# A head's loads in another order, cached keys on a semaphore of their own, value outputs copied in the MLP

## The chip, the cores and the metric

The kernel runs on one core of a Trainium2 chip. A core has five engines with instruction queues of their own: TensorE (PE, matrix products and transposes), VectorE (DVE), ScalarE (ACT), GpSimd (POOL) and SyncE (SP, which here only issues DMAs). They meet through semaphores. The metric is the device time of one launch in microseconds; the median of the runs before is 2062.98 us.

## What is computed

One layer of a streaming encoder, for a prompt of 1024 rows and a sample of 8 sequences with 16 new rows each, which share the weights. Four groups of four attention heads read the same projection; an output projection, an MLP and a gated embedding follow. Cut to the parts that the change touches:

```python
def _layer(h, p_l, past, ...):
    xn = _rmsnorm(h, g_attn)
    aq, ak, av, bq, bk, bv, cq, ck, cv, dq, dk, dv, dlogf = _project(xn, w_in, b_f)
    # past is None for the prompt; for the sample, cached keys and values stand in front:
    a_k = jnp.concatenate([a_past[:, :, 0], ak], axis=1)      # so for A, C, D; B has a window of 128
    a_v = jnp.concatenate([a_past[:, :, 1], av], axis=1)
    a_out = _stick_breaking(aq, a_k, a_v, q_pos, k_pos)        # A
    b_out = _swa_sample(bq, b_k, b_v, ..., sinks, rel_bias)    # B: softmax with a sink and a bias table
    c_out = _diff_attention(cq, c_k, c_v, ..., lam, rel_bias)  # C: two softmax maps and a bias table
    d_out = _forgetting_attention(dq, d_k, d_v, ..., f_q, f_k) # D: gates f added to the scores
    h = h + jnp.concatenate([a_out, b_out, c_out, d_out]) @ w_out
    h = h + jnp.square(jax.nn.relu(_rmsnorm(h, g_mlp) @ w_up)) @ w_down
    h = h + jax.nn.sigmoid(h @ w_ple_gate) * (p_l @ w_ple_proj)
    state = (stack([ak, av]), last window of [bk, bv], stack([ck, cv]), stack([dk, dv]), dlogf)
    return h, state
```

The new keys and values are outputs too (`a_kv_prompt`, `a_kv_sample` and so on); B's sample buffer is the old window moved on by 16 rows.

## The kernel before

The 1024 + 128 rows make nine tiles of 128 rows; the ninth is the sample. The program is a row of blocks, with a barrier of all engines between them: the projection, attention, the output projection, the MLP, the gated embedding. The projection leaves the turned queries and keys in DRAM, each as a high and a low part (`q2`, `k2`, cached keys `kc2`), and the values as rows (`vrows`).

Attention is a loop of two passes (`heads_loop`). A pass has eight jobs, `JOBS`: two heads each of A, B, C and D, an even and an odd one; a job has nine tiles. PE runs one tile ahead with the scores (`scores`), then turns the weights of the tile before, then multiplies by the values of the one before that. Each engine goes through its own list; what is not ready holds up all that stands behind it on that engine.

SP loads what a head needs into one of two buffers (`x = job % 2`), and starts when all outputs of the head two before are computed (L917). Its list for a head is, before the change: keys `k_turned` and queries `q_turned` in four arrangements, cached keys `k_sample_turned` (six and two loads; twelve and four for C, whose heads have two halves), with an even head the values `v_rows` and `v_cache_rows` of both heads of the group (semaphores `v_in`), and at the end the small ones: for B and C the bias of the prompt, eight loads of 9 KB with the sample's bias and one scalar a head (`head_scalar`); for D two loads of gates and eight of the sample's gates. All but the values count on one semaphore, `job_in0` or `job_in1`; `loads(g)` says how many there are. Three engines wait for its full count with `job_loaded`: DVE at the end of the seventh step of the head before (`bias`, or for D `sample_gates`), PE at a head's first scores, and GpSimd before it spreads the sample's queries and new keys (`spread_operands`).

Before the loop DVE casts two constants and clears two buffers (semaphore `att_zeros_set`), and GpSimd raises each of the loop's semaphores by one and then `att_primed`. SP and PE wait for both.

GpSimd also copies the new values from `vrows` to the outputs, DRAM to DRAM: nine copies a pass (`copies`), two behind a job's spreading. In the MLP it has nothing to do. There PE alternates products with `w_up` and `w_down`; SP loads their slots of 256 KB into four raw buffers, ACT and DVE split each into a high and a low part.

Of the kernel before, what the change touches and what calls it, by code (L numbers as in the profile page):

```python
# [19 lines left out]
F32 = mybir.dt.float32  # L20
# [5 lines left out]
P = 128  # L26
D = 1024
SEQ = 1024
# [4 lines left out]
HD = 64  # L33
# [29 lines left out]
def encoder(nc, i, o):  # L63
    with ExitStack() as ctx:
# [630 lines left out]
        with ExitStack() as mem:  # L695
            def sb(name, shape, dt=F32):
# [30 lines left out]
            a_set, kv_out = sem("att_zeros_set"), sem("kv_rows_out")  # L727
# [4 lines left out]
                "job_in0": "loads of the even head", "job_in1": "loads of the odd head",  # L732
                "turned": "PE: a bank of transposes is full", "v_in0": "loads of the values of a pair of heads of A or C",
# [80 lines left out]
            def loads(g):  # L814
                return (16 if g == "C" else 8) + {"A": 0, "B": 10, "C": 10, "D": 2 + DEC_B}[g]
# [14 lines left out]
            per["job_in1"] = 16 * sum(loads(g) for g, _ in JOBS[1::2])  # L830
            per.update({f"read{x}": len(range(x, len(ORDER), 3)) for x in range(3)})
# [71 lines left out]
            with nc.Block() as block:  # L903

                @block.sync
                def _(sp):
                    sp.wait_ge(primed_sem, 1)
                    sp.wait_ge(a_set, 4)

                    def body(j):  # L910
                        for job, (g, e) in enumerate(JOBS):
# [6 lines left out]
                            for m in range(HD // half):  # L918
                                own, at_hi, at_lo = bass.ds(HD * h + half * m, half), 2 * half * m, 2 * half * m + half
                                of_k = bass.ds(HD * kvh + half * m, half)  # L920
                                for part, to in ((0, at_hi), (1, at_lo)):
                                    sp.dma_start(kt[to:to + half, x, :].bitcast(F32), k2[g][part][of_k, :]).then_inc(done, 16)
                                    sp.dma_start(qt[0][to:to + half, x, :].bitcast(F32), q2[g][part][own, :]).then_inc(done, 16)
                                for part, to in ((1, at_hi), (0, at_lo)):
                                    sp.dma_start(qt[1][to:to + half, x, :].bitcast(F32), q2[g][part][own, :]).then_inc(done, 16)
                                for part, to in ((0, at_hi), (1, at_lo)):
                                    sp.dma_start(ks[to:to + half, x, :, 0:n].bitcast(F32),
                                                 kc2[g][part][of_k, :].rearrange("p (b n) -> p b n", b=DEC_B)).then_inc(done, 16)
                            if e == 0:
                                v, nb = GROUPS.index(g) % 2, DEC_B * cached(g)  # L930
                                w = HD if g == "B" else P
                                cache = i[f"cache_{g.lower()}_kv"]
                                vcol = 128 if g == "B" else 256
                                sp.wait_ge(q["o_full"], at("o_full", TILES * (job_of(GROUPS[GROUPS.index(g) - 2], 1) + 1) - (0 if g in "CD" else NT)))
                                sp.dma_start(vr[:, v, :, 0:w], vrows[:, bass.ds(V_COL[g] + w * j, w)].rearrange("(t p) d -> p t d", p=P)).then_inc(q[f"v_in{v}"], 16)
                                sp.dma_start(vc[:, v, 0:nb, 0:w], cache[:, bass.ds(vcol + w * j, w)].rearrange("(s p) d -> p s d", p=P)).then_inc(q[f"v_in{v}"], 16)
# [9 lines left out]
                            if g == "D":  # L946
                                sp.dma_start(cs[x][:, :], fcum_p[bass.ds(h, 1), :].partition_broadcast(P)).then_inc(done, 16)
                                sp.dma_start(fq[:, x, :], fcum_q[bass.ds(h, 1), :, :].rearrange("o p t -> (o p) t")).then_inc(done, 16)
                                for b in range(DEC_B):
                                    own = slice(b * DEC_S, (b + 1) * DEC_S)  # L950
                                    sp.dma_start(bs[own, x, :], fcum_s[b, bass.ds(h, 1), :].partition_broadcast(DEC_S)).then_inc(done, 16)
# [961 lines left out]
```

## Time and profile before

| | |
|---|---|
| runs | 2061.21, 2062.98, 2066.68 us; median 2062.98 us |
| the profiled execution | 2077.38 us, span 2075.8 us, mean granted PE clock 0.900 |
| busy in the span | PE 1839.8 us (89%), DVE 850.9 (41%), ACT 646.8 (31%), POOL 90.6 (4%) |
| DMA | 195.33 MB, 94 GB/s over the span |
| projection | to 338 us |
| attention, first pass | 366 to 656 us: PE busy 218.16 of 290 us, granted clock 0.69 |
| attention, second pass | 656 to 980 us: PE busy 246.18 of 324 us, granted clock 0.76 |
| MLP | 1123 to 1916 us |

The span runs from the first to the last instruction; the execution's own time is 1.6 us longer. The profiled execution is 14.4 us above the median of the runs without a profile. A row of the timeline gives in brackets how long its engine had been idle and what ended that. SPq is SP's queue: the time of such a row is that of the issue, not of the transfer; when the data has landed stands in the rows on DMA issues.

### The profile page before, as it was taken

Reading aid. Unit: us, or ns where it says so; the run is one execution under the profiler, and the core shown is the slowest. Engines: PE = TensorE matmul, PEld = TensorE weight load, DVE = VectorE, ACT = ScalarE, POOL = GpSimd, SP = SyncE. Lnnn points to the kernel's source line nnn. Section 1 sums busy time; section 2 is a strip of 40 time slices with the busy share of each in tenths; the row PEclk is TensorE's granted clock in tenths of the full one; section 3 lists DMA queues with packets and bytes.
Section 4 is the critical chain, followed back from the end, with each engine's and each line's share of the span. In section 5 each row is a group of like instructions: output and inputs, shape, how many; then the busy total and the mean of one; then the engine's idle time right before and its main releaser. Section 6 shows DMA issues by size and latency. Waiting matters only on the chain. (4 is left out here: it accounts for less than half of the span.)

```text
span 2075.8 us, 28346 instructions
## 1 busy us (share of the span) xinstructions
PE 1839.8 (89%) x10134; PEld 1659.4 (80%) x10134; DVE 850.9 (41%) x1619; ACT 646.8 (31%) x1387; POOL 90.6 (4%) x178
## 2 busy tenths in 40 slices
PE   6999995774888684788798999999999999999898
PEld 6999984674778574678688989999898999988686
DVE  4333322662455662455444333333333333333334
ACT  5322311552334552334223222222121212211326
POOL 0000000000011000010100000000000000000000
PEclk9999997676569686679899999999999999999899
DMA  5676733455347356354521111111111111110202
GB/s 170 211 245 221 250 140 77 106 120 125 65 106 162 77 115 133 65 114 93 191 95 36 41 50 47 52 49 46 45 41 41 41 41 41 41 41 21 87 28 94
DMA packets 152405, 195.33 MB, mean 94 GB/s; under 512 B 43188, under 2 KB 106356, under 8 KB 152248
## 3 DMA queue, kind: packets, MB, share of 16 engines
q1 hardware_dynamic: 105352, 131.63, 24.1%
q10 hardware_dynamic: 39136, 36.05, 5.3%
q0 software_dynamic: 7776, 25.76, 3.9%
q8 instruction: 88, 1.44, 0.3%
q14 instruction: 53, 0.43, 0.1%
HBM read 143.17 MB, written 54.81 MB: 95 GB/s over the span
## 5 line engine op out<-in xcount | busy, mean ns | idle before, releaser
L113 PE MATMUL up<-xt_hi,w_hi_even 128*128 128x384 f32 x768 | 258.2, 336 | 1.9 <-PEq L1426 1.8
L114 PE MATMUL up<-xt_lo,w_hi_even 128*128 128x384 f32 x768 | 257.8, 336 | 0.0
L115 PE MATMUL up<-xt_hi,w_lo_even 128*128 128x384 f32 x768 | 257.7, 336 | 0.0
L115 PE MATMUL down<-w_hi_odd_b,hidden_lo 128*128 128x512 f32 x576 | 224.6, 390 | 0.0
L114 PE MATMUL down<-w_lo_odd_b,hidden_hi 128*128 128x512 f32 x576 | 224.6, 390 | 0.0
L113 PE MATMUL down<-w_hi_odd_b,hidden_hi 128*128 128x512 f32 x576 | 224.2, 389 | 0.0
L1338 PE MATMUL scores<-k_turned,q_turned_straight 128*128 128x512 f32 (+5 forms) x224 | 87.7, 518 | 121.8 <-ACT probs L1060 68.8
L1633 DVE TENSOR_TENSOR h_rows<-down,h_rows 128x1024 f32<-128x1024 f32 x72 | 88.2, 1224 | 236.2 <-PE down L115 236.2
L1373 PE MATMUL outs<-v_rows,probs_turned 128*128 128x64 f32 x984 | 153.1, 307 | 35.0 <-DVE probs_turned L901 30.0
L1373 PEld LDWEIGHTS outs<-v_rows,probs_turned 128*128 128x128 f32 x984 | 145.5, 226 | 47.3 <-DVE head_out L1227 30.4
L1598 ACT ACTIVATE hidden_rows<-up 128x384 f32<-128x384 f32 x96 | 47.3, 492 | 417.2 <-PE up L115 417.2
L1338 PEld LDWEIGHTS scores<-k_turned,q_turned_straight 128*128 128x128 f32 (+1 forms) x224 | 44.1, 256 | 133.5 <-issue 72.1
L113 PEld LDWEIGHTS up<-xt_hi,w_hi_even 128*128 128x128 f32 x768 | 145.0, 189 | 3.8 <-DVE xt_lo L140 2.2
L114 PEld LDWEIGHTS up<-xt_lo,w_hi_even 128*128 128x128 f32 x768 | 144.9, 189 | 0.8
L1626 DVE TENSOR_TENSOR hidden_rows<-hidden_rows 128x384 f32<-128x384 f32 x96 | 53.6, 558 | 224.2 <-ACT hidden_rows L1598 224.2
L115 PEld LDWEIGHTS up<-xt_hi,w_lo_even 128*128 128x128 f32 x768 | 144.9, 189 | 0.0
L115 PEld LDWEIGHTS down<-w_hi_odd_b,hidden_lo 128*128 128x128 f32 x576 | 108.2, 188 | 22.5
L114 PEld LDWEIGHTS down<-w_lo_odd_b,hidden_hi 128*128 128x128 f32 x576 | 108.1, 188 | 22.0
L113 PEld LDWEIGHTS down<-w_hi_odd_b,hidden_hi 128*128 128x128 f32 x576 | 108.2, 188 | 21.9
L901 ACT COPY probs_turned<-turns 128x512 f32<-128x512 f32 (+3 forms) x156 | 68.3, 459 | 159.6 <-PE turns L1357 159.0
L1357 PE MATMUL turns<-cst,probs 128*128 128x128 f32 x520 | 101.9, 325 | 1.6 <-ACT probs L1046 1.6
L1177 DVE TENSOR_REDUCE stats<-scores 128x1 f32<-128x272 f32 (+8 forms) x76 | 51.5, 705 | 89.1 <-PE scores L1342 88.6
(262 smaller groups left out, 3539.4 us busy)
## 6 DMA issues: line engine op xcount, KB each, us to landing
w_raw<-w_up SPq DMA_DIRECT2D x64, 256.0 KB, 2.9
w_raw<-w_down SPq DMA_DIRECT2D x64, 256.0 KB, 3.0
w_raw<-w_in SPq DMA_DIRECT2D x24, 256.0 KB, 4.6
head_rows<-head_out ACTq DMA_DIRECT2D x16, 288.0 KB, 5.1
head_rows_in<-head_rows POOLq DMA_DIRECT2D x9, 512.0 KB, 4.7
x_rows<-x_prompt SPq DMA_DIRECT2D x8, 512.0 KB, 3.7
w_raw<-w_out SPq DMA_DIRECT2D x16, 256.0 KB, 5.0
residual_rows<-x_prompt POOLq DMA_DIRECT2D x16, 256.0 KB, 3.2
```

The source lines that it names most:

```text
L113: nc.tensor.matmul(out, xh, wh, start=first, stop=False)
L114: nc.tensor.matmul(out, xh, wl, start=False, stop=False)
L115: return nc.tensor.matmul(out, xl, wh, start=False, stop=last)
L901: copy(pt[i % 2][:, b * P:b * P + k], TB[n % 3][:, 0:k]).then_inc(q[f"read{n % 3}"], 1)
L1177: nc.vector.tensor_reduce(st_[:, col:col + 1], src[:, 0:n], AX.X, ALU.max, negate=True).then_inc(q["m_ready"], 1)
L1338: nc.tensor.matmul(S[UNIT[(i, m)] % 2][:, c:c + w], qt[part][own, e, P * t:P * (t + 1)], kt[own, e, k0 + c:k0 + c + w], start=part == 0, s ...
L1357: last = nc.tensor.transpose(TB[n % 3][:, (y - b) * P:(y - b + 1) * P], block_src, ident)
L1373: last = nc.tensor.matmul(dst, w[:, y * P:(y + 1) * P], vr[:, e, first_block(i) + y, own], start=y == 0, stop=y == nb - 1)
L1598: nc.scalar.activation(R[:, f % 2, :], U[f][:, 0:GT], ACT.Relu).then_inc(relu_d, 1)
L1626: nc.vector.tensor_tensor(R[:, f % 2, :], R[:, f % 2, :], R[:, f % 2, :], ALU.mult).then_inc(sq_d, 1)
L1633: nc.vector.tensor_tensor(H[:, t, :], DN[t % 2][:, :], H[:, t, :], ALU.add).then_inc(dn_add, 1)
```

## The change

SP's list for a head has a new order: the small loads first (bias and scalar, or gates), then keys and queries, then with an even head the values, and the cached keys last. The cached keys count on semaphores of their own, `ks_in0` and `ks_in1`. Only PE waits for these, before a head's sample tile; `loads(g)` loses their number, so DVE, GpSimd and PE at the head's start wait without them. SP no longer waits for `att_zeros_set`; GpSimd does, before its first spread. GpSimd's nine copies a pass become nine copies of whole tensors at the start of the MLP's block, and it waits for them at that block's end.

```diff
@@ per, semaphores @@
+                "ks_in0": "cached keys of the even head", "ks_in1": "cached keys of the odd head",
             def loads(g):
-                return (16 if g == "C" else 8) + {"A": 0, "B": 10, "C": 10, "D": 2 + DEC_B}[g]
+                return (12 if g == "C" else 6) + {"A": 0, "B": 10, "C": 10, "D": 2 + DEC_B}[g]
+            def cache_loads(g):
+                return 4 if g == "C" else 2
@@ SP @@
                     sp.wait_ge(primed_sem, 1)
-                    sp.wait_ge(a_set, 4)
...
                             sp.wait_ge(q["o_full"], at("o_full", TILES * (job - 1)))
-                            for m in range(HD // half):
-                                (keys, queries, then cached keys ks, all .then_inc(done, 16))
-                            if e == 0:
-                                (values)
                             if g in "BC":
                                 (bias of the prompt, of the sample, scalar)
                             if g == "D":
                                 (gates)
+                            for m in range(HD // half):
+                                (keys, queries, .then_inc(done, 16))
+                            if e == 0:
+                                (values)
+                            for m in range(HD // half):
+                                of_k, at_hi, at_lo = ...
+                                for part, to in ((0, at_hi), (1, at_lo)):
+                                    sp.dma_start(ks[to:to + half, x, :, 0:n].bitcast(F32),
+                                                 kc2[g][part][of_k, :].rearrange("p (b n) -> p b n", b=DEC_B)).then_inc(q[f"ks_in{x}"], 16)
@@ GpSimd in attention @@
                     pool.sem_inc(primed_sem, 1)
+                    pool.wait_ge(a_set, 4)
+                    pool.sem_inc(pool_passed, 1)
-                    def copies(j):
...
-                            for dst, src in rows_out[2 * job:2 * job + 2]:
-                                nc.gpsimd.dma_start(dst, src).then_inc(kv_out, 16)
-                    pool.wait_ge(kv_out, 2 * 16 * 9)
@@ PE, scores @@
                         if is_sample(i):
                             pe.wait_ge(q["spread"], at("spread", 3 * (job + 1)))
+                            pe.wait_ge(q[f"ks_in{e}"], at(f"ks_in{e}", 16 * sum(cache_loads(JOBS[x][0]) for x in range(e, job + 1, 2))))
@@ MLP @@
+                @block.gpsimd
+                def _(pool):
+                    for g in "ACD":
+                        own = slice(V_COL[g], V_COL[g] + 256)
+                        nc.gpsimd.dma_start(o[f"{g.lower()}_kv_prompt"][:, 256:512], vrows[0:SEQ, own]).then_inc(kv_out, 16)
+                        nc.gpsimd.dma_start(o[f"{g.lower()}_kv_sample"][:, 256:512], vrows[SEQ:SEQ + P, own]).then_inc(kv_out, 16)
+                    own = slice(V_COL["B"], V_COL["B"] + P)
+                    (b_kv_prompt from vrows, b_kv_sample from cache_b_kv and from vrows)
+                    pool.wait_ge(kv_out, 16 * 9)
```

SP at the start of attention, before: it waits for the cleared buffers and for the primer, then loads the first head of A, cached keys included.

```order
L843 UNCONDITIONAL_BRANCH [waits att_zeros_set,att_primed]
L843 ISA
L922 ISA [waits att_o_full]
L922 DMA k_turned<-k_turned_A_hi 64x1152
L923 DMA q_turned_straight<-q_turned_A_hi 64x1152
L922 DMA k_turned<-k_turned_A_lo 64x1152
L923 DMA q_turned_straight<-q_turned_A_lo 64x1152
L925 DMA q_turned_crossed<-q_turned_A_lo 64x1152
L925 DMA q_turned_crossed<-q_turned_A_hi 64x1152
L927 ISA
L927 DMA k_sample_turned<-k_cache_turned_A_hi 64x8x256
L927 DMA k_sample_turned<-k_cache_turned_A_lo 64x8x256
```

And now: it waits for the primer alone, and the values follow the queries.

```order
L848 UNCONDITIONAL_BRANCH [waits att_primed]
L848 ISA
L941 ISA [waits att_o_full]
L941 DMA k_turned<-k_turned_A_hi 64x1152
L942 DMA q_turned_straight<-q_turned_A_hi 64x1152
L941 DMA k_turned<-k_turned_A_lo 64x1152
L942 DMA q_turned_straight<-q_turned_A_lo 64x1152
L944 DMA q_turned_crossed<-q_turned_A_lo 64x1152
L944 DMA q_turned_crossed<-q_turned_A_hi 64x1152
L950 REGISTER_ALU
L951 ISA [waits att_o_full]
```

The wait for `att_zeros_set` is gone, and the two loads of `k_sample_turned` stand behind the values.

SP at the second head of B, before: the end of its list, from the second load of queries on, with the bias and the scalar at the end.

```order
L923 DMA q_turned_straight<-q_turned_B_hi 64x1152
L922 DMA k_turned<-k_turned_B_lo 64x1152
L923 DMA q_turned_straight<-q_turned_B_lo 64x1152
L925 DMA q_turned_crossed<-q_turned_B_lo 64x1152
L925 DMA q_turned_crossed<-q_turned_B_hi 64x1152
L927 DMA k_sample_turned<-k_cache_turned_B_hi 64x8x128
L927 DMA k_sample_turned<-k_cache_turned_B_lo 64x8x128
L940 ISA
L940 DMA bias_prompt<-bias_rows 128x256
L943 DMA bias_sample<-bias_rows 16x144 x8
L945 REGISTER_ALU
L945 DMA head_scalar<-swa_sinks 128x1
```

And now, from the bias on:

```order
L925 DMA bias_prompt<-bias_rows 128x256
L928 DMA bias_sample<-bias_rows 16x144 x8
L930 REGISTER_ALU
L930 DMA head_scalar<-swa_sinks 128x1
L941 DMA k_turned<-k_turned_B_hi 64x1152
L942 DMA q_turned_straight<-q_turned_B_hi 64x1152
L941 DMA k_turned<-k_turned_B_lo 64x1152
L942 DMA q_turned_straight<-q_turned_B_lo 64x1152
L944 DMA q_turned_crossed<-q_turned_B_lo 64x1152
L944 DMA q_turned_crossed<-q_turned_B_hi 64x1152
L956 DMA k_sample_turned<-k_cache_turned_B_hi 64x8x128
L956 DMA k_sample_turned<-k_cache_turned_B_lo 64x8x128
```

Ten small loads have moved in front of the six of keys and queries, and the cached keys to the end.

PE before the sample tile of the first head of A, before:

```order
L1373 MATMUL outs<-v_rows,probs_turned 128x64 x4
L1309 ISA
L1320 REGISTER_ALU [waits att_spread]
L1329 MATMUL scores<-k_sample_turned,q_sample_spread_straight 128x272 [waits att_a_logw]
L1329 MATMUL scores<-k_sample_turned,q_sample_spread_crossed 128x272
```

And now:

```order
L1363 MATMUL outs<-v_rows,probs_turned 128x64 x4
L1298 ISA
L1299 ISA [waits att_spread]
L1310 REGISTER_ALU [waits att_ks_in0]
L1319 MATMUL scores<-k_sample_turned,q_sample_spread_straight 128x272 [waits att_a_logw]
L1319 MATMUL scores<-k_sample_turned,q_sample_spread_crossed 128x272
```

One wait more stands in front of the tile's first product.

## Rows read from the trace of the kernel before

**Rows 1.** Waits of the whole run: who waited <- for whom: us, times, longest.

```profile
PE scores L1338 <- ACT probs L1060: 68.8, 28, 20.6
...
DVE bias_sample L1139 <- DMA head_scalar<-rel_bias: 37.2, 2, 20.0
...
PE scores L1338 <- DMA k_sample_turned<-k_cache_turned_A_lo: 28.2, 1, 28.2
...
PE scores L1338 <- DVE bias_prompt_lo L1146: 15.6, 2, 8.4
...
DVE bias_sample L1123 <- DMA bias_sample<-fcum_sample: 13.5, 2, 7.2
```

**Rows 2.** Stretches: their us, engines' busy us (x), PE clock, DMA share, GB/s.

```profile
510.00:556.00 46.00, 36.91 (x174) 31.40 (x176) 22.51 (x59) 15.94 (x43) 2.28 (x6) 0.50 0.39 84
...
1123.00:1916.00 793.00, 792.93 (x4023) 724.47 (x4024) 274.22 (x391) 167.23 (x320) 0.00 (x0) 1.00 0.13 43
```

**Rows 3.** Timeline, start of attention: start us, us, engine, line, operation [idle before].

```profile
347.66 1.98 DVE L1115 MEMSET q_sample_spread_crossed<- 128x2304 f32 x1 [0.43 <-issue]
...
350.09 0.59 SPq L922 DMA_DIRECT2D k_turned<-k_turned_A_hi  x1
...
353.31 0.55 SPq L925 DMA_DIRECT2D q_turned_crossed<-q_turned_A_hi  x1
...
356.18 5.27 SPq L936 DMA_DIRECT2D v_cache_rows<-cache_a_kv  x1
...
365.99 0.47 PE L1338 MATMUL scores<-k_turned,q_turned_straight 128*128 128x128 f32 x1 [28.16 <-DMA k_sample_turned<-k_cache_turned_A_lo]
...
374.40 0.68 PE L1373 MATMUL outs<-v_rows,probs_turned 128*128 128x64 f32 x2 [1.45 <-DVE probs_turned L901]
```

**Rows 4.** Source line 961, GpSimd's primer: ns, first and last start us.

```profile
L961 POOLq EVENT_SEMAPHORE  x1: 17/17/17, 348.4 to 348.4; - x1
```

**Rows 5.** DMA issues of that start: xcount, KB, us to landing.

```profile
q_turned_crossed<-q_turned_A_hi SPq DMA_DIRECT2D x1, 288.0 KB, 7.4
...
v_cache_rows<-cache_a_kv SPq DMA_DIRECT2D x1, 1024.0 KB, 15.5
```

**Rows 6.** Timeline, first head of C in the first pass.

```profile
480.91 0.32 SPq L922 DMA_DIRECT2D k_turned<-k_turned_C_hi  x1
...
507.12 0.29 DVE L1139 TENSOR_SCALAR bias_sample<-bias_sample,head_scalar 128x144 f32<-128x144 f32 x1 [19.99 <-DMA head_scalar<-rel_bias]
...
509.99 0.47 PE L1338 MATMUL scores<-k_turned,q_turned_straight 64*128 64x128 f32 x2 [20.55 <-ACT probs L1060]
```

**Rows 7.** Timeline and landing, second head of C in the first pass.

```profile
522.65 0.32 SPq L922 DMA_DIRECT2D k_turned<-k_turned_C_hi  x1
...
530.22 0.39 SPq L925 DMA_DIRECT2D q_turned_crossed<-q_turned_C_hi  x1
...
q_turned_crossed<-q_turned_C_hi SPq DMA_DIRECT2D x1, 144.0 KB, 6.5
```

**Rows 8.** Timeline, small loads, second head of C in the second pass.

```profile
845.57 0.42 SPq L940 DMA_DIRECT2D bias_prompt<-bias_rows  x1
...
849.89 0.35 SPq L945 DMA_DIRECT2D head_scalar<-rel_bias  x1
```

**Rows 9.** Timeline, second head of B in the first pass.

```profile
455.93 0.53 SPq L922 DMA_DIRECT2D k_turned<-k_turned_B_hi  x1
...
461.62 0.62 SPq L940 DMA_DIRECT2D bias_prompt<-bias_rows  x1
...
467.23 0.35 SPq L945 DMA_DIRECT2D head_scalar<-swa_sinks  x1
...
471.87 0.15 DVE L1136 TENSOR_SCALAR head_scalar_negated<-head_scalar 128x1 f32<-128x1 f32 x1 [9.34 <-DMA head_scalar<-swa_sinks]
```

**Rows 10.** DMA issues of the whole run: xcount, KB each, median us to landing.

```profile
a_kv_prompt<-value_rows POOLq DMA_DIRECT2D x2, 512.0 KB, 4.0
```

**Rows 11.** Timeline of ACT, first split of `w_down` in the MLP.

```profile
1143.39 1.14 ACT L106 CAST w_hi_odd_b<-w_raw 128x512 fp32r<-128x512 f32 x2
```

More of the change, by code:

```diff
@@ L830, in encoder @@
             per["job_in1"] = 16 * sum(loads(g) for g, _ in JOBS[1::2])
+            def cache_loads(g):
+                return 4 if g == "C" else 2
+            per.update({f"ks_in{x}": 16 * sum(cache_loads(g) for g, _ in JOBS[x::2]) for x in range(2)})
             per.update({f"read{x}": len(range(x, len(ORDER), 3)) for x in range(3)})
@@ L917, in body @@
                             sp.wait_ge(q["o_full"], at("o_full", TILES * (job - 1)))
-                            for m in range(HD // half):
[L919 to L928, printed above, removed]
-                            if e == 0:
[L930 to L936, printed above, removed]
                             if g in "BC":
@@ L951, in body @@
                                     sp.dma_start(bs[own, x, :], fcum_s[b, bass.ds(h, 1), :].partition_broadcast(DEC_S)).then_inc(done, 16)
+                            for m in range(HD // half):
+                                of_q, at_hi, at_lo = bass.ds(HD * h + half * m, half), 2 * half * m, 2 * half * m + half
+                                of_k = bass.ds(HD * kvh + half * m, half)
+                                for part, to in ((0, at_hi), (1, at_lo)):
+                                    sp.dma_start(kt[to:to + half, x, :].bitcast(F32), k2[g][part][of_k, :]).then_inc(done, 16)
+                                    sp.dma_start(qt[0][to:to + half, x, :].bitcast(F32), q2[g][part][of_q, :]).then_inc(done, 16)
+                                for part, to in ((1, at_hi), (0, at_lo)):
+                                    sp.dma_start(qt[1][to:to + half, x, :].bitcast(F32), q2[g][part][of_q, :]).then_inc(done, 16)
+                            if e == 0:
+                                v, nb = GROUPS.index(g) % 2, DEC_B * cached(g)
+                                w = HD if g == "B" else P
+                                cache = i[f"cache_{g.lower()}_kv"]
+                                vcol = 128 if g == "B" else 256
+                                sp.wait_ge(q["o_full"], at("o_full", TILES * (job_of(GROUPS[GROUPS.index(g) - 2], 1) + 1) - (0 if g in "CD" else NT)))
+                                sp.dma_start(vr[:, v, :, 0:w], vrows[:, bass.ds(V_COL[g] + w * j, w)].rearrange("(t p) d -> p t d", p=P)).then_inc(q[f"v_in{v}"], 16)
+                                sp.dma_start(vc[:, v, 0:nb, 0:w], cache[:, bass.ds(vcol + w * j, w)].rearrange("(s p) d -> p s d", p=P)).then_inc(q[f"v_in{v}"], 16)
+                            for m in range(HD // half):
+                                of_k, at_hi, at_lo = bass.ds(HD * kvh + half * m, half), 2 * half * m, 2 * half * m + half
+                                for part, to in ((0, at_hi), (1, at_lo)):
+                                    sp.dma_start(ks[to:to + half, x, :, 0:n].bitcast(F32),
+                                                 kc2[g][part][of_k, :].rearrange("p (b n) -> p b n", b=DEC_B)).then_inc(q[f"ks_in{x}"], 16)
                     heads_loop(sp, body)
@@ L1011, in body @@
                     def body(j):
-                        rows_out = list(copies(j))
                         for job in range(len(JOBS)):
```

18 lines of the change are left out of this document (6 added, 12 removed).

## The prediction, made before the changed kernel was run

> **What bounds the kernel now.** I read the waits first, for the whole run, because they say where TensorE (PE) stands still and what released it. In the MLP there is nothing to win: from 1123 to 1916 us PE is busy in 792.93 of 793.00 us at the full granted clock [rows 2]. The idle time lies in the attention stage, and three rows hold the long pieces [rows 1]: 28.2 us at its start, once, until a load of cached keys had landed; 15.6 us in two waits on the bias tiles; and 68.8 us behind ACT's exponentials, of which one wait alone is 20.6 us. DVE's own rows tell what stands behind the last two: it waits 37.2 us, twice, for C's `head_scalar`, the last load of a head, and 13.5 us, twice, for the gates of D.
>
> Then the timelines, to see which load ends each wait. At the start, SP's first issue (350.09) comes 0.45 us behind the end of DVE's second memset (347.66 + 1.98 = 349.64), and PE starts at 365.99 [rows 3]. At the first head of C, SP issues from 480.91 on, DVE gets through its wait of 19.99 us at 507.12, PE moves at 509.99 after 20.55 us [rows 6]. At the second head of B SP issues from 455.93, DVE goes on at 471.87 after 9.34 us [rows 9]. The rule behind all: DVE, GpSimd and PE wait for one semaphore that counts all loads of a head, and a head's first issue waits until the head two before it is done. After that first issue, only the order and length of the load list decide. So I price each place as "first issue to ready", before and after.
>
> **Part 1, the start.** Six loads of keys and queries are issued first; the last, at 353.31, takes 7.4 us to land: 360.7 [rows 3, 5], 10.6 us after the first issue. PE waited on until the cached keys had landed, 365.99, so the new semaphore takes 5.2 us off. SP no longer waits for the memsets, but for GpSimd's primer, which signals at 348.4 [rows 4]; with the same 0.45 us and two more increments in front I take 1.0 us earlier. Gain 6.2 us (5.2 if the memset was no gate, 6.4 if the increments cost nothing). What is late next: the values. `v_cache_rows`, issued at 356.18, landed 15.5 us later at 371.7 behind 1 MB of cached keys; without these (5.2 us) and 1.0 us earlier it lands at 365.5, and PE's first value product, at 374.40, moves to 368.2 [rows 3, 5]. 2.7 us to spare. The cached keys then land some 5 us after the values, and their tile is the ninth of the head: covered. The wait that GpSimd takes over lies before its first spread, which needs the queries anyway.
>
> **Part 2, first head of C, in both passes.** Before: ready 507.12 - 480.91 = 26.2 us after the first issue [rows 6]. After: ten small loads in front, then twelve of keys and queries. The small ones are priced by their issue: 849.89 + 0.35 - 845.57 = 4.7 us where the queue took them at once [rows 8], 467.23 + 0.35 - 461.62 = 6.0 us in the slower place [rows 9]. I take 5.3, because the queue is empty now but ACT's store of an earlier head is issued in the same microseconds. The twelve: the second head of C took from 522.65 to 530.22 + 6.5 = 536.7, 14.1 us, with one pair of cached keys among them [rows 7]. Such a pair of 256 KB is half of what took 5.2 us at the start, 2.6, so 11.5 us; up to 12.7 if the store slows them. New: 5.3 + 11.5 = 16.8 us against 26.2: 9.4 us. The second pass waited 37.2 - 20.0 = 17.2 us instead of 20.0 [rows 1], so I take 8.6 there. Together 18.0. PE's wait falls from 20.55 to some 11 us and does not vanish. Late next: values (1.6 MB, 8 us at the pace of 1 MB of cached keys in 5.2) land near 25 us after the first issue; PE wants them two tiles into the head, so they stay covered, and cached keys eight tiles in.
>
> **Part 3, second head of B, in both passes.** Before: 471.87 - 455.93 = 15.9 us [rows 9]. Here the small loads were issued under the transfers of the keys; in front, they stand alone. New: 5.3 + 10.6 (six loads as at the start; 11.3 at worst beside the store) = 15.9 to 16.6. A loss of 0.2 each, -0.4 us; the cached keys left out are 2 us that the small loads eat.
>
> **Part 4, the rest.** D: DVE's two waits of some 7 us [rows 1] stand in front of the maximum of a tile that PE is still working on, and PE's own waits list none behind them; 0 to 1 us, I take 0.5 for both. First head of B, second of A and of C: the waits come in twos, one a pass [rows 1], and none is theirs: nothing to gain, and part 3's 0.7 us more would not hurt. PE's added wait, 16 times, is a register instruction and a semaphore read: 0.5 us against. GpSimd's 18 copy issues in attention held up nobody that PE waits for: 0. The nine copies now start with the MLP. A copy of 512 KB landed in 4.0 us [rows 10]; 4480 KB make 35 us if one follows another. In these 35 us only `w_down` loads are needed, and the first split of them is at 1143.39, 20 us into the MLP [rows 11]: cover for a load that takes twice its time. If the next four come 3 us late too, ACT catches up in its idle time; bounds 0 to 6 us against, and I take 0, because PE reaches the first down product only after eight units of the up product.
>
> **Sum.** 6.2 + 18.0 - 0.4 + 0.5 - 0.5 = 23.8 us off the profiled execution's 2077.38: 2053.6. The runs shown have a median 0.7% below it (2062.98), so 2053.6 x 0.993 = **2039 us**, 1.2% faster. With the small loads at 4.7 or 6.0 us and the twelve at 12.7 this case reaches from 2036 to 2045.
>
> **Rivals.** Let b be the time by which the small loads hold up the keys; the sum above has b = 5.3 at four places (C and B, two passes each), so the gain is 23.8 + 4 x 5.3 - 4b = 45 - 4b.
>
> *The small loads cost more than their issue*: b = 8, for tiny rows that hold the queue. Gain 13, 2050 us. For it: from their first issue to the end of DVE's wait there were 10.25 us (461.62 to 471.87) [rows 9]. Against it: they stood behind 2.2 MB of keys, queries and cached keys there.
>
> *Slower: the small loads go one after another*, each paying its own way to landing before the keys move. The mechanism sits in SP's queue at every head of B, C and D; the point from which it decides is b = 11.3, where 45 - 4b is zero. One small load costs between 0.47 us (4.7 / 10, nothing but its issue) and 4.6 us (from the last issue, 467.23, to the end of DVE's wait, 471.87) [rows 8, 9]; at 2 us each ten make b = 20: 45 - 80, 35 us slower, 2098, with D's share not counted. Against it: ten are issued in 6.0 us, and 4.6 us after the last one all had landed [rows 9]; in a row that would leave a load 1.1 us. This is also where the Trainium skill speaks against the change: "DMA: Bandwidth & Descriptors", "Rules for kernel authors", says that transfers under 64 KB pay mostly overhead, and its section on the anatomy of one DMA fits a fixed cost of about 2 us to each (on GpSimd's path; these loads are SP's). Paid in a row, that would be this rival's 2098; the trace bears out an overhead in latency, not one that adds up.
>
> *The wait is only replaced*: C becomes ready earlier, but PE then stands for values, cached keys or the bias work on DVE, and only the start pays: 2057. Against: the cover worked out above.
>
> *The clock*: the head of C runs with the low level granted (0.50 over 510 to 556, PE busy 36.91 of 46 us) [rows 2]. If a wait of 11 us instead of 20 leaves it high for half of that head, some 4 us a head more, and the same at other places: 2031. Against: the wait stays long, and the head's own pauses, 9 of these 46 us, stay as they are.
>
> **Chances.** Forecast 0.70, dear small loads 0.14, clock 0.08, wait replaced 0.05, slower 0.03. The range 2030 to 2053 leaves out the last two and the far half of the second, some 0.15. What a measurement of this kernel can tell from no change is about 0.3%, 6 us, so faster means under 2057: 0.70 + 0.14 + 0.08 = 0.92; within 0.3% 0.05; slower 0.03.
>
> **What would show it.** SP's first issue near 349, PE's start near 359.8, released by queries and not by cached keys. DVE's wait for C near 10 us instead of 20 and 17; its wait at B still 9 us. PE's idle before the sample tiles not released by cached keys. PE as busy in the MLP as before. Wrong would be: keys that land later than 17.5 us after the first issue at C or 17 at B; values that end a wait of PE at the start; a gap in the MLP's first 40 us.

## The result, and the profile after

| | before | changed |
|---|---|---|
| median of 12 runs each on one chip | 2070.32 us (2059.40 to 2077.18) | 2049.65 us (2042.48 to 2056.34) |
| profiled execution | 2077.38 us | 2052.67 us |

The ratio is 0.991, 95% interval 0.989 to 0.9929: some 19 us, with 15 to 23 in the interval. The forecast was 2039 us and 23.8 us off the profiled execution; the pair of profiled executions lies 24.7 us apart, of which 1.7 us are the projection, which the change leaves alone (it ends at 336.16 instead of 337.83 us).

The waits of the changed kernel (who waited <- for whom: us, times, longest) answer to [rows 1]:

```profile
PE scores L1328 <- ACT probs L1049: 53.4, 28, 11.4
...
PE scores L1328 <- DMA q_turned_crossed<-q_turned_A_hi: 21.9, 1, 21.9
DVE bias_sample L1128 <- DMA q_turned_crossed<-q_turned_C_hi: 21.7, 2, 10.9
...
PE scores L1328 <- DVE bias_prompt_lo L1135: 14.2, 2, 7.1
...
DVE bias_sample L1112 <- DMA q_turned_crossed<-q_turned_D_hi: 4.9, 2, 2.5
```

Where a row names a load, the name has changed: what is last now are the queries, not the cached keys or the small loads. C's wait on DVE went from 37.2 to 21.7 us, D's from 13.5 to 4.9, PE's start from 28.2 to 21.9, and B's stayed (15.6 to 14.2).

The start, in the changed kernel's timeline and DMA issues (xcount, KB, us to landing), answers to [rows 3, 5]:

```profile
345.98 1.98 DVE L1104 MEMSET q_sample_spread_crossed<- 128x2304 f32 x1 [0.43 <-issue]
347.25 0.59 SPq L941 DMA_DIRECT2D k_turned<-k_turned_A_hi  x1
...
358.11 0.47 PE L1328 MATMUL scores<-k_turned,q_turned_straight 128*128 128x128 f32 x1 [21.95 <-DMA q_turned_crossed<-q_turned_A_hi]
...
366.54 0.68 PE L1363 MATMUL outs<-v_rows,probs_turned 128*128 128x64 f32 x2 [1.45 <-DVE probs_turned L906]
...
v_cache_rows<-cache_a_kv SPq DMA_DIRECT2D x1, 1024.0 KB, 12.0
...
q_turned_crossed<-q_turned_A_hi SPq DMA_DIRECT2D x1, 288.0 KB, 7.5
```

SP issues 0.7 us before the second memset has ended, not behind it. PE's first value product waits 1.45 us for DVE, to the hundredth as before: the cached values, issued at 351.91 and landed 12.0 us later at 363.9, came in time.

The first head of C and the second of B in the first pass (timeline), which answer to [rows 6, 9]:

```profile
477.61 0.35 SPq L925 DMA_DIRECT2D bias_prompt<-bias_rows  x1
...
483.04 0.38 SPq L941 DMA_DIRECT2D k_turned<-k_turned_C_hi  x1
...
494.53 0.29 DVE L1128 TENSOR_SCALAR bias_sample<-bias_sample,head_scalar 128x144 f32<-128x144 f32 x1 [10.87 <-DMA q_turned_crossed<-q_turned_C_hi]
...
497.39 0.48 PE L1328 MATMUL scores<-k_turned,q_turned_straight 64*128 64x128 f32 x2 [11.43 <-ACT probs L1049]
...
452.61 0.36 SPq L925 DMA_DIRECT2D bias_prompt<-bias_rows  x1
...
468.95 0.15 DVE L1125 TENSOR_SCALAR head_scalar_negated<-head_scalar 128x1 f32<-128x1 f32 x1 [8.02 <-DMA q_turned_crossed<-q_turned_B_hi]
```

C is ready 494.53 - 477.61 = 16.9 us after its first issue (forecast 16.8, before 26.2), B 468.95 - 452.61 = 16.3 (forecast 15.9 to 16.6, before 15.9). The small loads hold up the keys' first issue by 483.04 - 477.61 = 5.4 us at C (forecast 5.3; the same in the second pass) and by 5.8 and 5.7 at B.

A part of C's 26.2 us before is seen in SP's queue. There the small loads stood behind the load of 1 MB of cached values, and the first of them alone took 8 us to issue (7.81 in the second pass), against 0.35 now:

```profile
492.68 8.01 SPq L940 DMA_DIRECT2D bias_prompt<-bias_rows  x1
```

The MLP (windows: us, busy us of PE, PEld, DVE, ACT, POOL, clock, DMA share, GB/s), and its slowest copy:

```profile
1097.40:1891.00 793.60, 793.57 (x4026) 725.64 (x4027) 274.00 (x391) 167.08 (x320) 5.55 (x9) 1.00 0.15 49
...
w_raw<-w_down SPq DMA_DIRECT2D x4, 256.0 KB, 5.7
...
b_kv_sample<-value_rows POOLq DMA_DIRECT2D x1, 64.0 KB, 16.8
```

PE is as busy as in [rows 2]; the copies are done within 17 us of their issue, and the first loads of `w_down` beside them took 5.7 us without a gap behind it.

What the forecast has no term for is seen in windows of single heads. Before: the first heads of B in both passes (437 and 756), the first and second of C in the first pass.

```profile
437.20:463.80 26.60, 22.36 (x177) 21.30 (x175) 15.25 (x49) 11.82 (x38) 2.37 (x6) 0.87 0.34 86
488.40:559.00 70.60, 40.95 (x209) 35.09 (x207) 24.82 (x69) 16.97 (x47) 2.36 (x6) 0.53 0.50 105
559.00:610.30 51.30, 43.12 (x269) 37.91 (x267) 25.79 (x67) 18.88 (x52) 5.55 (x8) 0.63 0.45 102
755.90:778.10 22.20, 20.54 (x177) 19.44 (x175) 12.41 (x48) 11.41 (x38) 2.37 (x6) 0.92 0.45 114
```

The same four heads in the changed kernel:

```profile
429.50:462.20 32.70, 29.34 (x177) 28.61 (x175) 15.40 (x49) 11.56 (x38) 1.18 (x4) 0.63 0.15 34
484.90:543.50 58.60, 36.31 (x208) 31.43 (x207) 24.78 (x69) 17.00 (x47) 1.16 (x4) 0.62 0.63 132
543.50:591.20 47.70, 39.19 (x269) 34.44 (x267) 25.66 (x67) 18.91 (x52) 4.87 (x7) 0.71 0.49 108
733.30:765.90 32.60, 29.25 (x176) 28.52 (x175) 15.34 (x49) 11.57 (x38) 1.16 (x4) 0.63 0.16 34
```

The first head of B issues the same products, with 3.4 us of pauses in both passes against 4.2 and 1.7 before, but at a clock of 0.63 instead of 0.87 and 0.92: 6.1 and 10.4 us longer. C's heads run at a higher clock than before: without the wait, 70.60 - 20.55 = 50.1 us became 58.60 - 11.43 = 47.2 (in the second pass 49.5 became 47.2), and the second head's 51.30 became 47.70 (in the second pass it took 47.5 both times). Over attention both nearly cancel: without PE's idle time it took 469.3 us before and 470.8 after (from PE's first scores to its last output, less the idle time in front of each of its instructions in the timeline), while the idle time in it fell from 150.7 to 132.8.

### The profile page after: what moved, and what is told of

Read it like the earlier page. It is cut to its first block and busy times, and to the rows that moved or that the text cites. A ratio compares the mean times of both kernels' runs of the same rounds, so it can differ in the third digit from the quotient of the medians.

```text
span 2050.9 us, 28291 instructions
## 1 busy us (share of the span) xinstructions
PE 1840.6 (90%) x10134; PEld 1664.0 (81%) x10134; DVE 850.9 (41%) x1619; ACT 647.1 (32%) x1387; POOL 85.2 (4%) x169
## 3 DMA queue, kind: packets, MB, share of 16 engines
q1 hardware_dynamic: 105352, 131.63, 24.7%
## 5 line engine op out<-in xcount | busy, mean ns | idle before, releaser
L1363 PEld LDWEIGHTS outs<-v_rows,probs_turned 128*128 128x128 f32 x984 | 152.1, 235 | 44.1 <-DVE head_out L1216 27.8
L1363 PE MATMUL outs<-v_rows,probs_turned 128*128 128x64 f32 x984 | 158.8, 315 | 32.3 <-DVE probs_turned L906 27.4
L113 PEld LDWEIGHTS down<-w_hi_odd_b,hidden_hi 128*128 128x128 f32 x576 | 108.2, 188 | 21.9
```

Of the source, the lines that this page charges most:

```text
L113: nc.tensor.matmul(out, xh, wh, start=first, stop=False)
L1363: last = nc.tensor.matmul(dst, w[:, y * P:(y + 1) * P], vr[:, e, first_block(i) + y, own], start=y == 0, stop=y == nb - 1)
```

## The experiments

PE's four long waits are given for the second head of B and the first of C, each in the first and second pass. Ratios are to the kernel before, run beside each kernel on the same chip. There it took 2068.5 us (e1 to e4), 2065.7 (e5, e6, e7, e10), 2073.0 (e9, e11, e12) and 2067.0 (e13), so kernels of different groups are compared by their ratios and not by their medians.

| kernel | median us | ratio, interval | waits at B | at C |
|---|---|---|---|---|
| before | 2070.3 | 1 | 8.4, 7.2 | 20.6, 17.8 |
| changed | 2049.7 | 0.991, 0.989 to 0.9929 | 7.1, 7.0 | 11.4, 11.4 |
| e1 small loads last | 2061.2 | 0.997, 0.9946 to 0.9994 | 6.5, 7.8 | 19.5, 20.1 |
| e2 small loads in front, nothing else | 2068.8 | 0.9996, 0.9973 to 1.0019 | 10.7, 10.9 | 17.4, 15.3 |
| e3 copies in attention | 2043.8 | 0.9868, 0.9837 to 0.990 | 7.1, 6.9 | 11.6, 11.4 |
| e4 keys, then small | 2034.5 | 0.9818, 0.9787 to 0.9849 | 4.2, 6.0 | 8.8, 8.7 |
| e5 merged small loads | 2041.7 | 0.9883, 0.9844 to 0.9923 | 6.9, 4.3 | 6.2, 9.7 |
| e6 small loads' own semaphore | 2042.9 | 0.9895, 0.9862 to 0.9928 | 7.5, 5.2 | 8.9, 6.4 |
| e7 merged, own semaphore | 2035.9 | 0.9862, 0.9826 to 0.9897 | 4.9, 2.7 | 5.5, 7.0 |
| e9 keys, merged small, own semaphore | 2029.7 | 0.9817, 0.9781 to 0.9853 | 5.7, 3.3 | 7.0, 6.9 |
| e10 eight small loads more | 2058.4 | 0.9956, 0.9931 to 0.9981 | 11.2, 10.5 | 10.8, 11.0 |
| e11 unread products in the waits | 2048.4 | 0.9898, 0.9866 to 0.993 | 6.3, 6.0 | 6.2, 5.5 |
| e12 and in C's tiles | 2026.9 | 0.9796, 0.9759 to 0.9833 | 4.5, 6.3 | 6.1, 6.1 |
| e13 = e9 with those of C's tiles | 2009.2 | 0.9715, 0.9672 to 0.9759 | 4.8, 5.2 | 7.3, 7.0 |

**Which part pays: e1 and e2.** e1 is the changed kernel with the blocks of SP's list in another order:

```diff
-  small loads; keys and queries; values; cached keys
+  keys and queries; values; cached keys; small loads
```

> The changed kernel with the small loads put back to the end of a head's list (keys and queries, values, cached keys, small loads); start, semaphores and copies stay as changed. My theory (the order of the small loads pays at C, the start pays by the semaphore): PE starts as in the changed kernel, 21.9 us after the projection; at the first head of C all loads are in some 26 us after the first issue instead of 16.9, PE's wait there goes from 11.4 back to 18 to 21 us in both passes; B a little better than before (15.5 to 16). Time 6 to 8 us below the kernel before, 14 to 17 above the changed one, near 2064. Rival (the cached keys on a semaphore of their own are what pays at C, the place of the small loads does not matter): PE's wait at C stays near 11 us and the time within 4 us of the changed kernel.

e2 is the kernel before with the block `if g in "BC" ... if g == "D" ...` put in front of the keys.

> The kernel before with only the small loads put in front of a head's list; one semaphore, cached keys behind the keys, start and copies as before. My theory: PE's start as before (28 us); at the first head of C ready at 5.3 + 14.1 + 2.6 = 22 us after the first issue instead of 26, at the second head of B 5.3 + 10.6 + 2.6 = 18.5 instead of 15.9; the two nearly cancel, time 0 to 6 us below the kernel before. Rival (putting the small loads in front is the whole gain outside the start): 10 us or more below the kernel before, C ready at 17 to 18.

Waits on DVE in e1, and then in e2:

```profile
DVE bias_sample L1128 <- DMA head_scalar<-rel_bias: 38.4, 2, 19.5
...
DVE head_scalar_negated L1125 <- DMA head_scalar<-swa_sinks: 16.1, 2, 8.7
```

```profile
DVE bias_sample L1139 <- DMA k_sample_turned<-k_cache_turned_C_lo: 31.7, 2, 16.9
...
DVE head_scalar_negated L1136 <- DMA k_sample_turned<-k_cache_turned_B_lo: 23.5, 2, 11.8
```

In e1 C waits as before the change, and what is left is the start: 6 us by the ratio (1 to 11 in the interval), as expected. In e2 C is ready 22.9 us after its first issue (22 expected) and B 18.1 to 18.3 (18.5 expected): PE's wait at C falls by 2.4 to 3.1 us a pass and that at B grows by 2.3 to 3.7, and the sum is nothing. So neither the order of the small loads nor the own semaphore of the cached keys is the gain at C; it takes both, since whatever stands last on the semaphore ends the wait.

**The copies: e3** puts the nine copies a pass back into GpSimd's loop.

> The changed kernel with the value copies put back to GpSimd's list in attention (eighteen halves, two behind a head's spreading). My theory: the copies cost nothing at either place; time within 3 us of the changed kernel, PE's waits at B and C within 0.5 us of it. Rival (the copies' traffic lay on the loads of the heads, and moving them is a part of the gain): 4 to 10 us above the changed kernel, with PE's waits at B or C longer by 1 us or more each.

The four waits are the same within 0.2 us. By the ratios e3 is some 9 us shorter than the changed kernel, known to some 8 (by the two intervals), which neither its theory (within 3 us) nor its rival (longer) had. The waits do not show where that lies, and it stays open. What is shown is that putting the copies back into attention made nothing longer, so that moving them gained nothing.

**The price of the small loads: e4, e5, e10.** e4 changes the order once more; e5 makes one load of eight; e10 makes sixteen of eight at B and C.

```diff
 e4
-  small loads; keys and queries; values; cached keys
+  keys and queries; small loads; values; cached keys
 e5
-  for b in range(DEC_B):
-      sp.dma_start(bs[b * DEC_S:(b + 1) * DEC_S, x, 0:P + DEC_S], src[:, 0:P + DEC_S]).then_inc(done, 16)
+  sp.dma_start(bs[:, x, 0:P + DEC_S], src[:, 0:P + DEC_S].unsqueeze(0).broadcast_to((DEC_B, DEC_S, P + DEC_S))).then_inc(done, 16)
```

> The changed kernel with keys and queries first, then the small loads, then values, then cached keys. My theory (in front the small loads cost their issue time, 5 us, with the transfer engines idle; behind the keys their issue lies under the transfers): ready at B 13 us after the first issue instead of 16.3, at C 14 instead of 16.9; PE's four long waits lose 2 to 3.5 us each; time 8 to 13 us below the changed kernel. Rival (small rows queue behind the keys' data and land late, as at B before the change, 15.9 us): PE's waits within 1 us of the changed kernel, no difference that can be measured.

> The changed kernel with the eight loads of bias_sample made one (for B and C from the same 16 rows, for D from the eight sequences' gates): three small loads a head in front instead of ten. By my formula each place pays b, the issue time of the small loads: 3 x 0.47 = 1.4 us instead of 5.3, so ready at C 13 us after the first issue instead of 16.9, at B 12.4 instead of 16.3; PE's four long waits shrink by 3.5 to 4 us each; about 15 us below the changed kernel, 34 below the kernel before. Rival (the small loads cost latency, not issue time: the keys stand behind the landing of the last one): the wait shrinks by 1.5 us a place at most, 6 us in all. Second rival (one load that reads the same rows eight times is as long as the eight): no difference.

> The changed kernel with bias_sample at B and C loaded in sixteen loads of half the size: eight more issues in front of the keys, the same bytes. By my formula b grows by 8 x 0.47 = 3.8 us at four places: PE's waits at C 15 us, at B 11, 15 us above the changed kernel, near 2064. Rival (the small loads lie beside the keys' transfers and cost latency alone): within 4 us of the changed kernel.

e4's waits on DVE show the small loads last again, but sooner than the keys that stand behind them in the changed kernel:

```profile
DVE bias_sample L1128 <- DMA head_scalar<-rel_bias: 16.3, 2, 8.2
DVE head_scalar_negated L1125 <- DMA head_scalar<-swa_sinks: 11.9, 2, 6.9
```

At C the first issue stands at 473.99 and DVE goes on at 488.44: 14.4 us (expected 14); at B it is 13.9 and 14.3 (expected 13). PE's four waits lose 36.9 - 27.6 = 9.3 us together, and the ratio falls by 0.009, or 19 us, known to some 8: the small loads are better issued under the keys' transfers than ahead of them. They may stand behind the keys, but not behind the values and cached keys: e1, where they do, differs from e4 in that alone, and C is ready after 25.1 and 25.7 us there.

e10 stretches the issue at C from 5.4 to 7.3 us only:

```profile
472.90 0.36 SPq L925 DMA_DIRECT2D bias_prompt<-bias_rows  x1
...
480.21 0.35 SPq L941 DMA_DIRECT2D k_turned<-k_turned_C_hi  x1
...
491.17 0.29 DVE L1128 TENSOR_SCALAR bias_sample<-bias_sample,head_scalar 128x144 f32<-128x144 f32 x1 [10.26 <-DMA q_turned_crossed<-q_turned_C_hi]
```

A load of half the size was issued every 0.37 us instead of 0.46, so eight more cost 2 us and not 3.8. C was ready 491.17 - 472.90 = 18.3 us after its first issue, and 18.6 in the second pass (16.9 in the changed kernel), B 18.5 and 18.7 (16.3): 1.4 to 2.4 us later, where 3.8 were expected. PE's waits do not show this: at B they grew by 3.4 and 4.0 us and at C not at all, because PE ran dry at other moments (at C 10.3 us after the first issue instead of 8.4). By the ratios e10 is some 10 us longer than the changed kernel, known to some 7, between its theory's 15 and its rival's 4.

In e5 C was ready after 13.9 and 15.2 us (13 expected) and B after 13.8 in both passes (12.4 expected): 1.6 to 3.0 us sooner, where 3.9 were expected. The three small loads held up the keys by 1.7 to 2.0 us instead of 1.4, and the keys then took 11.9 to 13.5 us at C, instead of 11.5. The time, some 6 us below the changed kernel and known to some 9, decides between none of e5's three cases. So the formula's sign held at every place in e5 and e10, and its size came out at a third to three quarters. The Trainium skill, "DMA: Bandwidth & Descriptors", "Rules for kernel authors", says to coalesce many small transfers; the waits agree, with 27.1 us for the four in e5 against 36.9, while the interval of e5's ratio takes in the changed kernel's 0.991.

**A semaphore for the small loads: e6, e7, e9.**

```diff
-  .then_inc(done, 16)                    # small loads
+  .then_inc(q[f"sm_in{x}"], 16)
-  job_loaded(dve, job)
+  small_loaded(dve, job)                 # waits for sm_in alone
```

> The changed kernel, in its own order, with the small loads on semaphores of their own, for which alone DVE waits; GpSimd and PE wait for keys and queries as now. Theory: DVE gets through at 7 to 8 us after the first issue instead of 16.9, the bias and the last tile of the head before are done while the keys arrive, and PE starts when they land: its wait at C falls from 11.4 by the 2.9 us between DVE's release and PE's start to 8.5, at B from 7.1 by 1.4 to 5.7; 8 to 9 us below the changed kernel. Rival (what holds PE at C is the exponentials of the head before, not the keys): PE's wait at C falls to 3 us or less, 20 us below.

> Both: three small loads in front on semaphores of their own, keys and queries behind them. Keys land at 1.4 + 11.5 = 13 us after the first issue at C and 12.4 at B; PE runs dry 8.4 and 10.6 us after it, so its waits are 4.5 us at C and 1.8 at B, against 11.4 and 7.1: 4 x 6 = 24 us below the changed kernel, near 2025. Rival (the two gains are one and the same wait): no better than the merged loads alone, 15 us below.

> The order keys and queries, small loads, values, cached keys, with bias_sample in one load and the small loads on semaphores of their own, for which alone DVE waits. Keys land at 10.7 us after the first issue at C, the three small loads just behind them at 11 to 11.5: PE's wait at C 4 to 5 us, at B 1 to 3, against 11.4 and 7.1. About as good as merged small loads in front with their own semaphore, 2028 to 2036; rival (DVE passes its wait only when the last small load has landed, and PE waits for the bias tiles after that): C's wait 7 us or more, 2036 to 2042.

The waits of e6, and then of e7, name the keys' and queries' transfer itself:

```profile
PE scores L1338 <- DMA q_turned_crossed<-q_turned_C_hi: 15.3, 2, 8.9
PE scores L1338 <- DMA q_turned_crossed<-q_turned_B_hi: 12.6, 2, 7.5
...
DVE bias_sample L1138 <- DMA head_scalar<-rel_bias: 2.0, 1, 2.0
```

```profile
PE scores L1335 <- DMA q_turned_crossed<-q_turned_C_hi: 12.6, 2, 7.0
PE scores L1335 <- DMA q_turned_crossed<-q_turned_B_hi: 7.5, 2, 4.9
```

DVE's long waits at C are gone (21.7 us in the changed kernel, 2.0 in e6), and PE's wait there is 8.9 where 8.5 was expected: keys hold PE, not the exponentials behind DVE. In e9 the small loads are last again and DVE's wait at C is back (12.7 us, of which 6.4 at most); PE's four waits sum to 22.9 us in e9 and to 20.1 in e7.

The time followed the waits only roughly. Against the changed kernel, PE's idle time in attention fell by 12.4 us in e6, 17.8 in e7, 18.2 in e9 and 8.2 in e4; by the ratios the time fell by 3, 10, 19 and 19 us, each known to some 8. e6's 3 leaves its 8 to 9 open, e7 stays short of its 24; e9 has the time of its theory, but with the 7 us of wait at C that its rival gave. The idle time is read from one execution, and PE's own time differs beside it. Attention as a whole (windows as above), in the changed kernel, in e6 and in e9:

```profile
358.11:961.63 603.52, 470.75 (x3096) 425.47 (x3096) 328.32 (x799) 263.80 (x648) 33.88 (x76) 0.73 0.49 103
```

```profile
357.35:940.63 583.28, 462.91 (x3096) 415.81 (x3096) 329.54 (x799) 263.23 (x648) 34.14 (x76) 0.75 0.50 107
357.64:934.12 576.48, 461.91 (x3096) 414.13 (x3096) 328.91 (x799) 263.60 (x648) 33.90 (x76) 0.75 0.51 108
```

The same 3096 instructions kept PE busy for 470.75 us at a mean granted clock of 0.73, and for 462.91 and 461.91 us at 0.75. The runs of one kernel differ in the same way: e2's shortest took 2059.38 us at a mean clock of 0.919, its longest 2082.91 at 0.892. So what the waits leave over goes with the clock.

**The clock: e11, e12, e13.** Products of `ident` with `ident`, into a bank of the turns that is free at that moment, which nobody reads:

```diff
+  def idle(i, count):
+      x = WHERE[("tile", max(i - 2, 0), 0)]
+      wait_read(pe, x - 3)
+      for _ in range(count):
+          nc.tensor.matmul(TB[x % 3][:, 0:P], ident, ident, start=True, stop=True, skip_group_check=True)
   def scores(i):
+      if g == "C" and t > 0:                                         # e12, e13
+          idle(i, 3)
+      if t == 0 and (g, e) in (("A", 0), ("B", 1), ("C", 0)):        # e11, e12
+          idle(i, {"A": 24, "B": 12, "C": 24}[g])
```

> The changed kernel with products that nobody reads on PE in its long waits: 24 of 128x128 before the first head of A, 12 before the second of B, 24 before the first of C, into a bank of the turns that is free then (0.27 us each at the full clock, 0.42 at half: 6 to 10 us, within the waits). Nothing else is changed, the waits themselves end when they did. Theory (the rise and fall of the granted clock, set off by the waits, is what moves the rest of attention by 10 to 15 us from run to run and kernel to kernel): the heads behind a filled wait run at a higher clock, 0.62 in the first head of C goes over 0.75, attention without PE's idle time falls from 471 by 8 to 15 us, the total by as much. Rival (a head's clock is set by its own short pauses): 0.55 to 0.68 there again, total within 4 us of the changed kernel.

> The one before with three such products more in front of each tile of C but the first (32 tiles in all, 0.8 us a tile at the full clock, 1.3 at half), where PE pauses 1.1 to 2 us a tile. Theory (a tile's pauses hold the clock of C down): C's heads run at 0.9 to 1.0 instead of 0.62 and 0.71 and take 40 us or less instead of 47 without the long wait: 20 to 30 us less in all for the four. Rival (the clock stays low, the products cost their time beyond the pauses): C's heads are 3 to 8 us longer each, total 10 to 30 us more.

> The kernel with keys and queries first, three small loads on semaphores of their own, values, cached keys, and before each tile of C but the first the three products that nobody reads; none in the long waits. Theory (the products hold the clock of C by themselves, and the two gains lie at different places): C's heads at 0.9 to 1.0 and 5 to 7 us shorter each than without them, in all 20 to 25 us less than the kernel without them (2029.7), 2005 to 2012. Rival (the clock of C was raised by the products in the waits ahead of it): C's heads at 0.6 to 0.7, 10 to 30 us more than without them.

The two heads of C in the first pass, in e11, then e12, then e9, then e13 (windows as above):

```profile
474.60:533.30 58.70, 41.62 (x256) 36.68 (x254) 24.77 (x69) 17.00 (x47) 1.17 (x4) 0.68 0.63 128
533.30:581.00 47.70, 39.19 (x269) 34.43 (x267) 25.65 (x67) 18.90 (x52) 4.89 (x7) 0.71 0.49 108
```

```profile
483.60:534.70 51.10, 38.34 (x304) 34.15 (x303) 24.67 (x69) 17.00 (x47) 1.17 (x4) 0.90 0.72 147
534.70:576.70 42.00, 35.18 (x316) 31.27 (x314) 25.56 (x67) 18.91 (x52) 4.87 (x7) 1.00 0.56 123
```

```profile
472.00:527.10 55.10, 37.82 (x208) 32.52 (x207) 24.76 (x69) 16.97 (x47) 1.16 (x4) 0.60 0.59 122
527.10:574.60 47.50, 39.14 (x269) 34.39 (x267) 25.64 (x67) 18.88 (x52) 4.87 (x7) 0.71 0.51 109
```

```profile
481.10:529.70 48.60, 35.05 (x256) 30.68 (x254) 24.59 (x69) 16.99 (x47) 1.17 (x4) 0.82 0.66 136
529.70:572.70 43.00, 36.84 (x317) 32.63 (x315) 25.56 (x67) 18.91 (x52) 4.88 (x7) 0.96 0.57 121
```

e11 goes to its rival. Before its first scores PE stood still for 12.2 us, did the products from 347.53 on and waited 2.0 us more, instead of 21.9 in one piece; C's heads ran at 0.68 and 0.71 (0.62 and 0.71 in the changed kernel, without the products) and took 58.7 and 47.7 us, as in the changed kernel. The total is the changed kernel's too. e12 goes to the theory: with three products more a tile (each is two instructions in the rows), the second head of C makes 316 instructions in 42.0 us at the full clock, where 269 took 47.7 at 0.71, and PE's busy time falls from 39.2 to 35.2 us with 47 instructions more. 42.0 is more than the 40 us that were expected, and the total lies 21 us below e11's by the ratios, known to some 10. So the pauses between C's tiles (up to 2.0 us in the changed kernel, none over 1.3 with the products) held its clock down, and not the wait ahead of the head. Whether the length of a pause counts or how much PE does in a tile as a whole, these runs do not tell apart. e13 adds this to e9: 2009.2 us, by the ratios 21 below e9 and known to some 12, as expected, and the best of all kernels here.

## Why the prediction was right, step by step

- *Start.* 6.2 forecast, 28.16 - 21.95 = 6.2 measured. Both parts hold. From the end of the projection to the first issue it took 11.1 us instead of 12.3, and the issue came before the memset's end: 1.2 (forecast 1.0). From there to PE's start it took 10.9 instead of 15.9, and the queries ended the wait: 5.0 (forecast 5.2). The values were not late.
- *First head of C.* The ready time was right: 16.8 forecast, 16.9 measured in both passes. So was the gain from the first issue to PE's start: 29.1 us became 19.8 in the first pass and 28.3 became 19.7 in the second, 9.3 and 8.6 less (forecast 9.4 and 8.6). PE's wait, which the sum took for the same thing, fell by 9.1 and by 6.4: 15.5 instead of 18.0. The mis-sized term is the wait of the second pass. A wait has two ends: before, PE ran dry 10.6 us after the first issue there (795.02 to 805.57); the head ahead of it ran at a clock of 0.68. In the changed kernel it was 8.4 us (781.33 to 789.69), at 0.77. PE arrived 2.2 us sooner, and waited as much longer. The total lost nothing by that, for the head ahead took 3.7 us less. The windows of that head, before and then changed:

```profile
778.10:804.50 26.40, 18.76 (x118) 18.11 (x117) 9.69 (x49) 9.41 (x37) 2.37 (x6) 0.68 0.62 136
```

```profile
765.90:788.60 22.70, 15.22 (x118) 14.59 (x118) 9.53 (x49) 9.51 (x37) 1.16 (x4) 0.77 0.51 102
```

- *Second head of B.* Ready at 16.3 in both passes as forecast, and PE's start came 0.4 and 0.7 us later after the first issue than before. But PE's wait became shorter by 1.3 and 0.2 us instead of longer by 0.4 in all. It is the same thing turned round: the head ahead was at 0.63, and PE came late to its wait, 10.6 us after the first issue in both passes instead of 8.9 and 9.8.
- *Sample tiles, D, copies, added waits.* No wait of PE names the cached keys. DVE's wait for D's gates fell by 8.6 us, and the 0.5 us booked for it are not to be seen, as PE's own waits list none behind it. The copies cost nothing in attention, as e3 shows from the other side, and PE stayed busy beside them in the MLP. PE's waits before the sample tiles, behind GpSimd and ACT, sum to 12.7 us and were 11.0; no run shows the 0.5 us for the added semaphore by itself.
- *Rivals.* Dear small loads (b = 8) gave 2050, which is the time that was measured; that is chance, for b was 5.4 at C and 5.7 to 5.8 at B, and the distance to 2039 lies elsewhere, as the next point says. Loads that go one after another fell: C's keys landed 11.5 us after their own first issue, as forecast without small loads in front. A wait that is only replaced fell: 23 us of idle time left PE. The clock's rival was half right: the first head of C gained 2.9 and 2.3 us from it (4 forecast) and the second 3.6 in the first pass and nothing in the other, but the first head of B lost 16.5 over both passes, which no case had.
- *The time.* All terms sum to 23.8 us; the waits in the profile give 6.2 + 15.5 + 1.5 = 23.2. The runs give 15 to 23. The 2049.65 us lie in the range, but above the likeliest case's own 2036 to 2045: 7 us of that are the kernel before, which ran at 2070.3 in twelve runs and at 2063.0 in the three from which the forecast was scaled.

By medians the change gives 20.7 us, so some 3 us of the sum stay open. The first head of B took 20.9 to 26.6 us in some profiles (both passes of the kernel before, of e2, e6, e9, e10 and e11) and 30.7 to 32.7 in others (both passes of the changed kernel, of e3 and e4, one of e1, e5, e7, e12 and e13), with the same products. Whether the new order makes the long form more frequent can't be told from one profile a kernel, and no experiment here settles it.

## What to carry to other kernels

When several loads count on one semaphore, the last one is the wait: look first for what its reader does not need yet, and give that a semaphore of its own; moving other loads ahead of it gained nothing by itself here (e2). Price a place as "first issue to ready", and the wait as the distance from there to when the waiting engine runs dry, because that end moves too; e10's waits at C did not grow although its loads landed later. Look also for a small load that stands behind a large one in the same queue: before the change, one such issue took 8 of the 26 us until C was ready. And where an engine's granted clock is low in a stretch, shortening a wait ahead of it may leave the stretch as slow as it was; the pauses inside it are what to look at.

## What was not expected of the hardware

- Work that nobody reads made the kernel faster: 96 products in C's tiles took some 20 us off (e13 against e9, and e12 against e11); the granted clock of C's heads rose with them from 0.60 and 0.71 to 0.82 and 0.96, and the heads became 6.5 and 4.5 us shorter in the first pass.
- With PE busy in 29.3 of 32.7 us, the clock was 0.63 (the first head of B in the changed kernel); with 20.5 of 22.2 it was 0.92. The products were the same.
- Issuing a load from SP cost 0.37 us at 4.5 KB and 0.46 at 9 KB a load. Right behind a load of cached values of 1 MB an issue took far longer:

```profile
351.91 0.49 SPq L952 DMA_DIRECT2D v_cache_rows<-cache_a_kv  x1
352.59 7.18 SPq L956 DMA_DIRECT2D k_sample_turned<-k_cache_turned_A_hi  x1
```

With the values in front of them, the cached keys are held up in the queue itself, which nothing here waited for. Before the change the small loads of C stood there (8.01 us, shown above), and DVE and PE waited for them.
